# A fused two-block model on one core: first stage joined to the projection, gate tiles last, scan written out, output stage's first tiles by planes

## The reference

```python
# conditioning: six vectors of 1024, mod = silu(c) @ w_ada + b_ada
h = rms_norm(x) * (1 + scale) + shift
z, xbc, dt_raw, u = split(h @ w_in)          # 768, 1792, 12, 256 columns
xbc = silu(causal_depthwise_conv(xbc, conv_w, conv_b))   # 4 taps
xs, bm, cm = split(xbc, [768, 1280])         # 12 heads of 64; 4 groups of 128 states
dt = softplus(dt_raw + dt_bias); a = -exp(a_log)
# scan in 8 chunks of 128 tokens, a_cs the running sum of dt*a in a chunk
decay = exp(where(causal, a_cs[l] - a_cs[s], -inf))
y = (C B^T * decay) (xs*dt) + exp(a_cs) * (C state)
state = state * exp(a_cs[-1]) + B^T (xs*dt*exp(a_cs[-1] - a_cs))
y = (y + xs * d_skip) * silu(z)
y = rms_norm(y by groups) * norm_w
mix = concat(pool_mixer(u), y) @ w_out       # pool: trailing means less the token
```

## Time and profile before

| what | us |
|---|---|
| median of 3 runs (lowest to highest) | 2485.39 (2485.37 to 2487.03) |
| profiled execution, its own time | 2484.32 |
| its span on the core | 2482.5 |
| PE busy in the span | 2151.3 (87%) |
| DVE busy | 1264.1 |
| ACT busy | 802.7 |
| POOL busy | 630.7 |

### The profile page before, as it was taken

One profiled execution on the slowest core, in us unless ns is written; L12 is line 12 of the kernel. 1 busy time (PEld: TensorE's weight loads), 2 busy tenths in 40 slices (PEclk: granted clock), 3 DMA queues, 4 the chain that ended last, 5 costly groups with the idle time before them and its releaser, 6 DMA issues. The chain is left out here.

```text
span 2482.5 us, 43484 instructions
## 1 busy us (share of the span) xinstructions
PE 2151.3 (87%) x15844; PEld 1617.9 (65%) x15844; DVE 1264.1 (51%) x1550; ACT 802.7 (32%) x1107; POOL 630.7 (25%) x412
## 2 busy tenths in 40 slices
PE   4599976689565897898986898989999999999998
PEld 3488855468432453454545786768888888888887
DVE  2777259842434686786875446844433123311334
ACT  4222123220243676786863104732101001100113
POOL 4133315511000000000003362213333323323334
PEclk6799987779677898998996899999999999999999
DMA  5533303431899997899954220011111111111113
GB/s 208 188 109 126 129 34 120 146 119 60 348 409 411 367 342 269 347 353 339 343 218 164 77 93 13 1 43 51 43 51 49 45 51 51 42 51 51 42 59 119
DMA packets 106317, 377.33 MB, mean 152 GB/s; under 512 B 8108, under 2 KB 19212, under 8 KB 105868
## 3 DMA queue, kind: packets, MB, share of 16 engines
q1 hardware_dynamic: 87772, 333.46, 37.0%
q10 hardware_dynamic: 13008, 23.07, 2.5%
q0 software_dynamic: 5472, 19.93, 2.2%
HBM read 344.92 MB, written 31.51 MB: 152 GB/s over the span
## 5 line engine op out<-in xcount | busy, mean ns | idle before, releaser
L1573 PE MATMUL moe_hu<-x_res,moe_xt 128*32 128x256 f32 x5120 | 337.0, 407 | 80.0 <-DVE moe_xt L1489 51.5
L1467 DVE COPY x_res<-moew_raw 128x2048 f32 x243 | 270.4, 1137 | 184.1 <-DMA moew_raw<-in_w 109.8
L1573 PEld LDWEIGHTS moe_hu<-x_res,moe_xt 128*32 128x32 f32 x5120 | 162.6, 115 | 210.3 <-issue 86.4
L240 PE MATMUL ff_acc<-ff_yh,ff_w_hi 128*128 128x512 f32 x704 | 274.4, 390 | 0.0
L240 PE MATMUL ff_acc<-ff_yl,ff_w_hi 128*128 128x512 f32 x704 | 273.9, 389 | 0.0
L240 PE MATMUL ff_acc<-ff_yh,ff_w_lo 128*128 128x512 f32 x704 | 273.9, 389 | 0.0
L1467 ACT ACTIVATE x_res<-moew_raw 128x2048 f32 (+1 forms) x121 | 197.2, 1630 | 105.4 <-DMA moew_raw<-in_w 66.9
L208 POOL CAST ff_w_hi<-ff_w_raw 128x1024 fp32r<-128x1024 f32 (+1 forms) x82 | 82.1, 1001 | 546.5 <-PE ff_acc L240 546.5
L240 PE MATMUL ff_acc<-xh,ff_w_hi 128*128 128x512 f32 x480 | 188.2, 392 | 8.1 <-DVE ff_w_lo L224 7.4
L210 POOL TENSOR_TENSOR ff_w_lo<-ff_w_raw,ff_w_hi 128x1024 fp32r<-128x1024 f32 (+1 forms) x82 | 189.1, 2306 | 6.6
L240 PE MATMUL ff_acc<-xl,ff_w_hi 128*128 128x512 f32 x480 | 187.3, 390 | 0.0
(11 more groups left out here) (376 smaller groups left out, 3783.2 us busy)
## 6 DMA issues: line engine op xcount, KB each, us to landing
moew_raw<-in_w SPq DMA_DIRECT2D x192, 1024.0 KB
ff_w_raw<-in_w_up SPq DMA_DIRECT2D x44, 512.0 KB, 3.5
mid_w_raw<-in_w_qkv SPq DMA_DIRECT2D x24, 512.0 KB, 3.5
in_w_raw<-in_w_in SPq DMA_DIRECT2D x23, 512.0 KB, 3.5
x_res<-in_w_ada SPq DMA_DIRECT2D x20, 512.0 KB, 5.1
y_scratch<-acc_sq ACTq DMA_DIRECT2D x80, 128.0 KB
ff_w_raw<-in_w_down SPq DMA_DIRECT2D x16, 512.0 KB, 3.4
ssd_m<-acs_scratch SPq DMA_DIRECT2D x8, 768.0 KB, 3.9
```

The lines of the kernel that those rows point to most:

```text
L240: m = pe.matmul(o, w[:, b, k * P:(k + 1) * P], x[:, k, h:h + HALF], start=(k == 0 and t == 0), stop=(k == kt - 1 and t == 2))
L1467: m = e.activation(to, src, ACT.Copy) if k == "act" else e.tensor_copy(to, src)
L1573: m = e.matmul(hu[u % 2][rows(j), 0:2 * FW].rearrange("p (a f) -> p a f", a=2), xt[:, t, rows(u)], w[:, :, FW * j:FW * (j + 1)], start=(t ...
```

## The change

**A.** `prepare` is gone; its work stands at the head of `mixer_in`, without the barrier and the second load of c. Each x tile is turned once. 1/rms is spread over partitions by one matmul with a diagonal for each token half (`diagonal`, `spread_root`). DVE scales a plane and adds nothing (`scaled`), ACT adds the shift as it rounds (`high`), DVE makes `low`. Twenty `w_ada` tiles are taken here and four a pass in the conv loop, which has seven passes. The first two weight tiles are multiplied plane by plane in the order `FIRST`, the second `LAG` planes behind the first.

```diff
+FIRST = ((0, 0), (0, 1), (0, 2), (0, 3), (0, 4), (1, 0), (1, 1), (1, 2), (1, 3), (1, 4)) + tuple((h, k) for k in range(5, KT) for h in range(2))
+LAG = 4
...
+                    for b in range(2):
+                        g.load(e, 0, 2, b, W[2 + b])
+                    st.wait(e, st.act, f"raw{NT - 1}")
+                    e.dma_start(self.xt_dram, x[:, :, :]).then_inc(self.s_xout, 16)
+                    e.wait_ge(self.s_xout, 16)
+                    st.wait(e, st.dve, "scaled%d%d" % FIRST[-1])
+                    with e.Fori(0, N_SILU) as i:
+                        ada_load(e, i)
                         for b in range(2):
-                            g.load(e, i, 2, b, W[2 * i + (2 + b)])
-                        e.wait_ge(self.s_xout, 16)
-                        ada_load(e, i)
-                    ada_load(e, N_SILU + N_Z - 1)
+                            g.load(e, i, 4, b, W[2 * i + (4 + b)])
```

On PE the eight turnings and both spreads stand ahead of the first product:

```diff
+                    def product(b, h, k):
+                        for t, (w, v) in enumerate(((g.hi, self.xh), (g.hi, self.xl), (g.lo, self.xh))):
+                            m = e.matmul(g.acc[b][:, halves[h]], w[:, b, k * P:(k + 1) * P], v[:, k, halves[h]],
+                                         start=(k == 0 and t == 0), stop=(k == KT - 1 and t == 2))
...
+                    turn_raw(6, "raw4")
+                    turn_raw(7, "raw5")
+                    spread_root(1, "raw6")
+                    e.wait_ge(g.s_split, 4)
+                    for n in range(len(FIRST) + LAG):
+                        if n < len(FIRST):
+                            st.wait(e, st.dve, "lo%d%d" % FIRST[n])
+                            m = product(0, *FIRST[n])
+                            if n == len(FIRST) - 1:
+                                m.then_inc(g.s_mult, 1)
+                        if n >= LAG:
+                            m = product(1, *FIRST[n - LAG])
+                    m.then_inc(g.s_mult, 1)
+                    with e.Fori(0, N_SILU - 1) as i:
                         for b in range(2):
```

On ACT and DVE:

```diff
+                    def high(n):
+                        h, k = FIRST[n]
+                        st.wait(e, st.dve, f"scaled{h}{k}")
+                        st.act(e.activation(self.xh[:, k, halves[h]], tmp[n % 4], ACT.Identity, bias=self.mod[:, k:k + 1]), f"hi{h}{k}")
...
                     for j in range(POOL_T):
+                        gate(1 + j)
                         for h in range(2):
                             st.wait(e, st.pe, f"pool{j}{h}")
-                            st.act(e.activation(self.xh[:, j, h * HALF:(h + 1) * HALF], mix[h][:, :], ACT.Copy,
...
+                            st.act(e.activation(wrk[:, j, h * HALF:(h + 1) * HALF], mix[h][:, :], ACT.Copy,
+                                                scale=self.col("pool_scale", j)), f"pool_out{j}{h}")
+                    for n in range(1 + POOL_T, SSD_T - 1):
+                        gate(n)
+                    g.ready(e, 0, *side(LAST - 1))
+                    for j in range(POOL_T):
+                        for h in halves:
+                            st.act(e.activation(self.xh[:, j, h], wrk[:, j, h], ACT.Copy), f"pool_hi{j}{h.start // HALF}")
+                    gate(SSD_T - 1)
```

```diff
+                    def scaled(n):
+                        h, k = FIRST[n]
+                        st.wait(e, st.act, f"spread{h}")
+                        st.wait(e, st.dve, f"mod{k}")
+                        st.dve(e.scalar_tensor_tensor(tmp[n % 4], x[:, k, halves[h]], self.mod[:, KT + k:KT + k + 1], rbc[:, halves[h]],
+                                                      ALU.mult, ALU.mult), f"scaled{h}{k}")
...
+                    def low(n):
+                        h, k = FIRST[n]
+                        st.wait(e, st.act, f"hi{h}{k}")
+                        st.dve(e.scalar_tensor_tensor(self.xl[:, k, halves[h]], tmp[n % 4], self.mod[:, k:k + 1],
+                                                      self.xh[:, k, halves[h]].bitcast(F32), ALU.add, ALU.subtract), f"lo{h}{k}")
...
+                    for n in range(4, len(FIRST)):
+                        h, k = FIRST[n]
+                        if h == 0 and k > 5:
+                            ada(2 * k)
+                            ada(2 * k + 1)
+                            biased(k)
+                        scaled(n)
+                        if n > 4:
+                            low(n - 1)
+                    low(len(FIRST) - 1)
+                    for n in range(2 * KT, len(order)):
+                        ada(n)
```

**C.** The scan's loop is written out. POOL makes `skip` (the identity times `d_skip`) once and `xdte` in each chunk. PE turns from `xbc` directly and adds the skip term by a matmul (L976) for each pair of heads:

```diff
+                                    d_skip.unsqueeze(2).to_broadcast([P, SSD_T, P]), ALU.mult).then_inc(s_skip, 1)
+                    for c in range(NCH):
                         wait(e, "dte", c)
...
+                            at = slice(h // 2 * CH, h // 2 * CH + CH)
+                            k = e.matmul(xy[:, at], skip[:, h // 2, :], xbc[:, h // 2, cols(c)], start=True, stop=False)
+                            for w, x, last in ((xdt, m[b], False), (state, ce[b], True)):
...
+                                    k = e.matmul(xy[HD * j:HD * (j + 1), at], w[:, (h + j) * HD:(h + j + 1) * HD], x[:, (h + j) * CH:(h + j + 1) * CH],
+                                                 start=False, stop=last)
```

```diff
+                        wait(e, "dte_arg", c)
+                        for h in range(HEADS):
+                            a = m[b][:, h * CH:(h + 1) * CH]
+                            k = e.activation(a, a, ACT.Relu, bias=chunk(self.acs_tok, c)[:, h:h + 1], scale=-1.0)
+                        done(k, "below")
+                        done(e.activation(dte[:, b, :], dte[:, b, :], ACT.Exp), "dte")
+                        spread(e, s_bc, c)
                         done(e.activation(ce[b], ce[b], ACT.Exp), "exp_bc")
...
-                        done(e.activation(dte[:, b, :], dte[:, b, :], ACT.Exp), "dte")
                         wait(e, "exp_bc", c)
                         done(e.activation(cdec[:, b, :], heads(ce[b], CH)[:, :, CH - 1], ACT.Copy), "cdec")
-                        wait(e, "seg", c)
-                        done(e.activation(m[b], m[b], ACT.Exp), "exp_seg")
...
+                        wait(e, "gated", c)
+                        done(e.activation(zs[:, :, cols(c)], xbc[:, SSD_T:2 * SSD_T, cols(c)], ACT.Square), "squared")
```

```diff
                         done(e.tensor_tensor(dte[:, b, :], heads(m[b], CH)[:, :, CH - 1], chunk(self.acs_tok, c), ALU.subtract), "dte_arg")
-                        wait(e, "dte_arg", c)
-                        done(e.tensor_tensor(heads(m[b], CH), heads(m[b], CH), per_head(chunk(self.acs_tok, c), CH), ALU.min), "min")
...
+                    for c in range(NCH):
+                        if c + 1 < NCH:
+                            decay_c(c + 1)
                         wait(e, "y", c)
+                        done(e.tensor_tensor(xbc[:, SSD_T:2 * SSD_T, cols(c)], planes(xy[:, 0:SSD_T * P]), zs[:, :, cols(c)], ALU.mult), "gated")
                         wait(e, "state", c - 1)
-                        done(e.tensor_tensor(heads(state[:, :], HD), heads(state[:, :], HD), per_head(cdec[:, b, :], HD), ALU.mult), "decayed")
+                        done(e.tensor_tensor(heads(state[:, :], HD), heads(state[:, :], HD), per_head(cdec[:, c % 2, :], HD), ALU.mult), "decayed")
...
                         done(e.tensor_tensor(s2, s2, new_states, ALU.add), "state")
-                        if more:
+                        if c + 1 < NCH:
                             x_dt(c + 1)
-                    e.memset(state[:, :], 0.0).then_inc(s_state0, 1)
-                    e.memset(zeros, 0.0).then_inc(s_zeros, 1)
-                    e.wait_ge(s_state0, 1)
-                    x_dt(0)
-                    arguments(0, 0)
-                    decay_cb(0, 0)
-                    chunks(e, body)
+                        if c + 2 < NCH:
+                            arguments(c + 2)
```

```diff
+                    first_products()
+                    st.wait(e, st.pool, "wide")
...
+                    for k in range(2, KT):
+                        g.mult(e, k // 2, 0, k % 2, self.xh, self.xl)
+                        if k == 2:
+                            route(0)
+                        route(k - 1)
                     st.pe(route(KT - 1), "logits")
...
-                    for j in range(SSD_T):
-                        st.wait(e, st.dve, f"gated{j}")
-                        st.act(e.activation(zs[:, j, :], xbc[:, SSD_T + j, :], ACT.Square), f"gate_sq{j}")
                     e.preload_act_table(ACT.Sqrt)
+                    e.wait_ge(self.s_w_first, 32)
+                    for b in range(2):
+                        e.activation(g.hi[:, b, :], self.w_first[:, b, :], ACT.Copy).then_inc(g.s_first, 1)
...
+                    e.sem_inc(g.s_split, 2)
+                    for b in range(2):
+                        e.wait_ge(g.s_first, b + 1)
```

(1 more changed line is left out.)

609 lines of the change are left out of this document (287 added, 322 removed).

## The result

The changed kernel takes 2442.34 us (median of 4, 2440.75 to 2446.38); the kernel before, in the same comparison, 2486.21 (2485.37 to 2487.23). The ratio is 0.9826, with a 95% interval of 0.9809 to 0.9843: 44 us less in the medians, 43.0 in the profiled spans. The forecast was 2431, in a range of 2415 to 2446. The profiled execution took 2441.31 us with a span of 2439.5; forecast were 2430.1 and 2428.3.

What follows compares the result with a forecast made beforehand. Only the first 622 us are touched; there the bound changes four times, among them PE full in the projection and DVE in the scan. −32.3 − 10.9 + 3.4 − 14.4 = −54.2 gave 2431 us, range 2415 to 2446.

Steps and rivals of the forecast that it cites:

- Part A: Front: PE idles 17 us after its third tile, behind the x store's landing; tile 3 starts at 92.3; −32.3 us.
- Part B: Tile order, up to the scan's first transfer: 7.0 inline plus 3.6 after the last product against 21.5; −10.9 us.
- Part C: Scan: chunk 14.25 against 13.43 us, six periods +4.9, start −2.8, end +1.3; +3.4 us.
- S + 7.8: Scan chunk: ACT's chain, which DVE's ce products wait for, ends 7.8 us after a state's end S.
- Part D: Output stage, last state to first output product: 22.4 against 36.8, planes bring nothing; −14.4 us.
- if anything after 622 us moves with it: Sign of being wrong: only the first 622 us are touched, so the stretch after them should not move.
- Rival 1: Front: no wait, tile 3 follows tile 2 at 75; 19.6 us less, 2412; chance 0.10.
- Rival 2: Scan dearer by ACT: Relu step 0.386, longer exp, chunk 15.5, slow start; 2441 us; chance 0.15.
- Rival 3: Scan cheaper: Relu step 0.22 takes 0.84 us off each chunk; 2423 us; chance 0.13.
- Rival 4: Scan: ce products stay slow since Pool isn't the cause; 3.9 us more a chunk, 2458; chance 0.05.
- rival 5: Slower than before through the scan's Relu chain: a step of 0.94 in place of 0.29, 2485 us; chance 0.02.
- rival 6: Front: planes don't start the first tiles early; tiles 0 and 1 end near 64, already in the sum; no chance given.

Runs made afterwards that it cites:

- e1: Changed kernel with the four modulation products of each conv-loop pass on DVE placed behind both convolutions, not ahead of them; 2429.2 us.
- e2: Changed kernel with the 4 MB store of x issued by ACT behind the last raw copy, no longer by SP behind the last first-stage weight tiles; 2433.0 us.
- e11: The kernel of e1 once more, for a second profile; 2430.2 us.
- e7: Changed kernel with the edits of e1, e3 and e4 together; 2409.3 us.
- e4: Changed kernel with the twelve Relu taken off ACT and made as twelve small 128x128 min instructions on DVE behind dte_arg; 2434.9 us.
- e3: Changed kernel with a chunk's six skip matmuls issued together ahead of the waits for ce and m, not one ahead of each head pair; 2443.1 us.
- e5: Changed kernel without the six skip matmuls of each chunk, so the output lacks a term and only the scan is read; 2454.6 us.
- e6: Changed kernel with the output stage's first two tiles multiplied whole, one after the other, not by planes with a lag of four; 2446.2 us.
- e12: The kernel of e7 once more; 2418.4 us.

## Why the prediction was right, and where it was off

It foresaw the sign, the new wait and its chain, the bound of the scan, and came out 11 us too low: 2431 against 2442, inside the range. In two of the parts sizes that were off cancelled, so their totals are better than their terms. By its steps:

**Part A** held to 2 us, in part by luck. Store issued at 58.3 (56), landed after 15.9 (15.7), first product at 78.2 (77.9), tile 3 from 94.3 (92.3). Within it some sizes were off against each other: the store was issued 2.3 later, the loads took 3.7 to DVE's first product where I had 6.1, the four products 6.4 for 5.1, as the third tile came 1.4 late, and conv(0) 7.6 for 7.0. e1 takes the wait away by order alone and e2 by an earlier store, so its cause is shown. What I did not see is that it was worth less than its length: with it gone, e1's first transfer gained 6.0 us in one profile and e11's 15.4 in the other. I had written of "little margin" between DVE's 21 us a pass and PE's 21.76. In the worse of its two courses DVE needs some 22.3 (e1's convolutions start at 90.5 and 112.8), in the better one it keeps PE's 21.76 (e7's start at 126.2 and 147.9), and without the hole at tile 3 PE is early enough to wait for it.

**Part B** held: −10.9 forecast, −10.6 measured; behind the last product 3.5 us in place of 21.5, and the inline work 7.4 us (321.5 less 94.3 is 227.2, 20 tiles of 10.88 are 217.6, the low clock 2.2).

**Part C** was the term with the wrong size, +8.2 for +3.4. Six periods were right (14.12 at the mean for 14.25: +4.1 for +4.9), and so were its parts: a Relu step of 0.29 ((3.60 − 0.39) / 11), ce at S + 7.8, ce products of 0.55. The rule of the Trainium skill, page "ScalarE: Activation LUTs", section "Rules for kernel authors", that sends min and relu to VectorE is borne out by e4: done there, the same step takes 2.3 us off each chunk. What failed is the price of the skip matmuls, "six full-width skip matmuls of 0.2 to 0.43 and the gate on DVE add 1.3", at the end only. By themselves they are near that size, 0.45 each at the low clock in e3's single run of six. Put between the pairs each lengthens its pair by 0.91 at the low clock (1.78 − 0.87) and 0.57 at the full one, and they stand in the first chunk's way as well: the start was +1.6 for −2.8, the end +2.5 for +1.3. Without them (e5) the start is 2.4 under the kernel before, near the −2.8 forecast, and the last chunk 0.5 under it. Why a skip costs more between two pairs than in a row of its own, no run here takes apart.

**Part D** came out at −14.7 for −14.4, by two errors that cancel (group sums 2.8 us shorter, weight splitting still in the way); e6 shows the planes to bring nothing, as said.

**The rest**, +4.3, was not foreseen, and the edits don't reach it. It would have been one of the prediction's own signs of being wrong ("if anything after 622 us moves with it"), but it does not exceed what one program shows by itself. The stretch from the first output product on lasted 1964.1 to 1974.9 in the eleven profiled runs that compute the full result, 1964.1 and 1973.0 for one and the same program (e1, e11), most of it in the expert stage (622.4 to 628.7). The kernel before, at 1964.5, has only one profile. Some 1.2 us between attention's last exponential and the feed-forward part's first silu (131.2 before, 132.4 to 132.8 in every later profile) look systematic; what causes them stays open. So some 4 of the 11 us are scatter or unexplained, 5 are the scan (the skip matmuls cost a little more than that, and the periods came out 0.8 shorter than forecast), 2 the front.

**The rivals.** Rival 1 (no wait) didn't come. Rival 2 named 2441, all but the measured time, and that is chance: its Relu step of 0.386 and chunk of 15.5 measured 0.29 and 14.1. Rival 3 (a step of 0.22) fails by the same rows; its own time should read 2425, as seven chunks of 0.84 are 5.9. Rival 4 (slow ce) is refuted by 548 to 559 ns; rival 5 was far off; rival 6, already in the sum, came as said, with tile 1 done at 67.0.

## What to carry to other kernels

When a wait is removed, ask which engine was nearly as late: here DVE was, and in one of two courses 9 of 15 us came back as a new wait. An instruction put on PE "beside other work" costs its full length in the first and last pass of a loop, where nothing is beside it, and at the low clock. Order matters too: the six skips added 0.91 us each between the pairs and took 0.45 each in one piece, during a wait. A small elementwise step belongs on the engine that idles just then: the same twelve operations took 3.6 us in ACT's chain, and each chunk was 2.3 us shorter with them in DVE's gap, though they take up to 3.7 us there.

## What the runs showed of the hardware that was not expected

One program falls into either of two courses from one execution to the next. DVE's 42 two-input taps take 56.4 us in e7 and e11 and 82.9 in e1 and e12, the 14 first taps 26.8 or 14.4, POOL's subtraction 2.5 or 3.0 at the mean, and the scan starts at 309 or 319. e2 has the worse course too (82.2). The changed kernel itself has 1.36 us a tap. What tips an execution to one side was not found. Single-input DVE instructions are longer beside POOL's too (0.81 alone, 2.77 beside the subtraction). How long PE's low clock lasts in the same program differs as well: the last chunk took 14.97 us in e1 and 11.91 in e11, one kernel, with all six pairs of heads at 1.78 us in the first and only two of them in the second.
